# Two edits of a schedule: cached states decayed one by one and loaded in four parts, sample-value products in twos

## The chip, the cores and the metric

The kernel runs on one core of one Trainium2 chip. The metric is the time of one execution on the device in microseconds (us). The core has five engines, each with its own instruction stream worked off in program order: TensorE (PE in the profile, its weight loads as PEld), VectorE (DVE), ScalarE (ACT), GpSimd (POOL) and SyncE (SP), which here mostly issues the DMA transfers. The engines meet through semaphores that the kernel sets and waits for by hand.

## The reference

One inference step of a trunk of two layers, for two groups of requests that share the weights: a prompt of 512 tokens, and 8 samples with 4 new tokens each (32 rows) and cached state. All of it is fp32.

```python
def trunk(x, past_even, past_odd, params):          # called for the prompt and for the samples
    for layer in range(DEPTH):                      # DEPTH = 2
        hn = rmsnorm(x, norm_mix[layer])
        if layer % 2 == 0: mix, st = even_mixer(...)
        else:              mix, st = odd_mixer(hn, odd_w_in[li], odd_w_out[li], past)
        x = x + mix
        hn = rmsnorm(x, norm_mlp[layer])
        x = x + jnp.square(jax.nn.relu(hn @ w_up[layer])) @ w_down[layer]

def ssd_scan(x, dt, a, bm, cm, h0):                 # in even_mixer, chunks of 128 steps
    ...
    def step(h, inp):
        da, s_c = inp
        return h * da[..., None, None] + s_c, h     # the state decays, then the chunk's part is added
    h_last, h_in = lax.scan(step, h0, (exp(acum[:, :, -1]), st))
    y = y + jnp.einsum('bclgn,cbghpn->bclghp', cm, h_in) * jnp.exp(acum)[..., None]

def window_attn_sample(q, k_cat, v_cat, n_past, dil, slopes, sink):   # in odd_mixer, dil = 1, 4, 16
    idx = n_past + jnp.arange(t_len)[:, None] - dil * steps[None, :]
    kg, vg = k_cat[:, idx], v_cat[:, idx]           # cached keys and values gathered by stride
    scores = jnp.einsum('btkgd,btjkd->btkgj', q, kg) * dh ** -0.5 + bias
    p, lse = softmax_lse(scores, sink)
    return jnp.einsum('btkgj,btjkd->btkgd', p, vg), lse
```

Each of the 8 samples has a cached scan state `state_ssm` of 32 heads x 64 x 128, in four groups of 8 heads. In layer 1 the three patterns' results are merged by their softmax denominators.

## The kernel before

**Big products.** Every projection is computed transposed, weights as the stationary operand, 512 + 32 columns as two halves of 272 (`HALF`). Each fp32 product is split into three (high x high, low x high, high x low), which gives six matmuls for one 128 x 128 block of weights. Eight such blocks make a chunk, in a PSUM tile `gp`. The kernel's time is laid out by these chunks: one chunk is a *slot* (`z`), one block in it a *place* (`part`, 0 to 7). All other work is woven in "beside" it: at a place, TensorE issues the six matmuls and then what the tables list for this place; the other engines walk the same tables.

**The scan (lines 115 to 165, `ssd_events`).** During the projection of the query and gate weights (24 slots, 192 places) the scan of layer 0 runs beside it in 20 steps, `SSD[T] = (g, c)`: for each group g of 8 heads first `c == 4`, the samples, which take 14 places from `W = SSD_W[T]` on, then the prompt's four chunks, 7 places each. For `c == 4` the state of all eight samples lies in `hs_t` (128 partitions x 8 samples x 512, 2 MB). TensorE multiplies c by it (`c_times_h`, line 2360) at W and W+1, which needs the loaded states (`hs_in`); its `y_of_sample` (line 2375) comes at W+4; from W+5 on comes one state product per place and sample (`state_of`, line 2389, its matmul line 2403), into one of two PSUM banks in turn. On VectorE, in the order of the tables: `c_h_out` at W+1, samples 0 to 3 of `hs_t` times their decay at W+2 (`decay_of_sample`, line 1708, its instruction line 1713), `y_out_of` at W+4, samples 4 to 7 at W+5, and from W+5 on one addition of a state product to a sample's state per place (`state_of_sample`, line 1716, its instruction line 1719). The state product of sample b waits for the addition of sample b-2 (line 2391), since they share a bank. `st.link(m)` makes VectorE's next instructions wait until m has been written. Between these lie VectorE's other duties: the mask product `m` (line 1658), the chunk's drain (`chunk_out`), x products, weight splits, and gate products (line 1589) of the groups. GpSimd does `c_exp` (lines 2846, 2849) and, per chunk, copies and masks that wait for the row transfers `heads` (line 785). SyncE stores the states at W+14 and loads the next group's at W+22, in one DMA of 2 MB (`load_states`, line 794).

**Layer 1 (lines 286 to 350).** The projection and output products run over 88 slots, in four quarters qd of four heads each, from `SLOT0 = (0, 18, 38, 58)`. The prompt's pieces (scores, turn, values) come at every slot of a quarter. The samples' values are read from the cache as *units*: `unit(U)` = (qd, half, g, t): 18 units a quarter, nine for samples 0 to 3 (half 0) and nine for samples 4 to 7. A unit is one 0.5 MB load of a value tile `vs` (`load_v`, line 958, the DMA's line 973) and one *set* of four products of probabilities and values (`times_unit`, line 2748; line 2759, eight records in the trace). In quarters 0 to 2 there are two value tiles (`N_RING`), in the last 15; a load into a tile waits until the set that used it is done. `sample_units` (line 293) gives each unit its place, every `per` places; each place is followed by one set. From these places follow: `SUM_AT`, where VectorE sums a finished half (`sum_v`, line 2168; it copies the half out of PSUM), `SB_AT`, where the half is turned and split into the operand of the output product (`sb`: TensorE products, ScalarE's `b_hi`, VectorE's `b_lo` on line 2165), and `LOAD_AT`, at which of three turns of a slot SyncE issues each load. The queue order of SyncE in a slot is: value loads of the turns early and mid, one key item (`load_item`, line 945, which itself waits for GpSimd's product of an earlier item), a weight group, value loads of the late turn, a second key item.

**Small products.** `small_events` places the small jobs of a quarter: `rq`, `rk`, `rv` (rows of the samples' queries, keys, values turned by TensorE, line 2697), `vt`, `mg`, `sb` and so on. They share one PSUM bank, and each job's TensorE part waits until the job before it in the table is drained (`small_done`). On VectorE, `factors_out` (line 2123, its copies line 2139) for quarter qd is emitted at the end of slot SLOT0 + 27; the next slot begins with the chunk's drain and, in every other slot, the weight split (line 1999).

## Time and profile before

The median of the three runs is 2426.38 us (2424.07 to 2429.6). The rows below and in the last section but one come from one profiled execution.

| | |
|---|---|
| time of the profiled execution | 2428.49 us |
| span from the first to the last instruction | 2426.7 us, 41530 instructions |
| granted TensorE clock, mean | 0.963 of full speed |
| TensorE matmuls (PE) busy | 2250.9 us, 93% |
| weight loads (PEld), beside them | 2101.6 us, 87% |
| VectorE | 1383.7 us, 57% |
| ScalarE | 730.9 us, 30% |
| GpSimd | 430.0 us, 18% |
| chain that ended last | PE 69%, DVE 12%, DMA 7%, issue 5%, ACT 4%, POOL 2% |
| DMA | 519.92 MB, mean 214 GB/s, best of the 40 slices 324 GB/s |

The chain that ended last is followed back from the last instruction, at each step to what released it. A share of 69% for TensorE says that for the rest of the span something else decided when the next TensorE instruction could start. Busy shares are means over stages with different limits: in the scan VectorE has far more to do per slot than in the MLPs.

### The profile page before, as it was taken

The page shows a single profiled execution, that of the slowest core. Times are in us where ns is not written, and L with a number is a line of the kernel's source. Part 1 is how long each engine was busy: PE and PEld are TensorE (multiplying, and loading weights), DVE is VectorE, ACT ScalarE, POOL GpSimd, SP SyncE. Part 2 cuts the span into 40 slices and gives each one's busy share as a digit, 9 for nine tenths or more (in the row PEclk, how much of TensorE's full clock was granted, in tenths as well). Part 3 has the DMA queues.
Part 4 walks back from the last instruction along what each step waited for, and adds up shares of the span by engine and source line. Part 5 has one row for each costly group of instructions (what it writes and reads, how often), then busy time and mean ns, then how long its engine had stood idle before and what let it go on. Part 6 is the DMA issues. An engine that isn't in the chain of part 4 may idle for free.

```text
span 2426.7 us, 41530 instructions
## 1 busy us (share of the span) xinstructions
PE 2250.9 (93%) x17512; PEld 2101.6 (87%) x17512; DVE 1383.7 (57%) x2005; ACT 730.9 (30%) x1408; POOL 430.0 (18%) x287
## 2 busy tenths in 40 slices
PE   7998887888899999999999999999999979999997
PEld 7988776677688999999998987898898858999997
DVE  4786777785644544344565564665646647353444
ACT  3323324355333322122313322323232224221221
POOL 1000322211121100000035434244324400000000
PEclk9999998888999999999999999999999989999999
DMA  4225766771233687787758668569657945877874
GB/s 164 70 81 179 242 242 229 263 234 62 79 134 121 227 269 260 260 276 252 252 165 300 223 225 297 167 199 313 215 172 254 324 156 173 271 264 246 278 260 176
DMA packets 282909, 519.92 MB, mean 214 GB/s; under 512 B 17776, under 2 KB 253664, under 8 KB 278880
## 3 DMA queue, kind: packets, MB, share of 16 engines
q1 hardware_dynamic: 271408, 324.44, 40.9%
q10 hardware_dynamic: 5888, 177.91, 20.0%
q0 software_dynamic: 5440, 15.08, 1.7%
q8 instruction: 131, 2.15, 0.4%
q14 instruction: 42, 0.34, 0.0%
HBM read 483.76 MB, written 210.80 MB: 286 GB/s over the span
## 4 chain that ended last, share of the span: by engine, by line
PE 69%; DVE 12%; DMA 7%; issue 5%; ACT 4%; POOL 2%; SPq 0%; DVEq 0%; ACTq 0%; POOLq 0%
PE gp L2264 33%; PE gp L2797 14%; PE gp L2593 5%; PE gp L2417 4%; DMA uk<-in_dil_k 3%; DVE cacc L1556 2%; DMA decay<-tmp_a_row 2%; PE mp L2684 2%; POOL uq L2897 1%; DMA vs<-in_dil_v 1%; PE mp L2653 1%; PE mp L2759 1%; PE mp L2515 1%; ACT w_hi L1004 1%; PE mp L2533 1%
## 5 line engine op out<-in xcount | busy, mean ns | idle before, releaser
L2264 PE MATMUL gp<-a_hi,w_hi 128*128 128x272 f32 x1456 | 307.0, 292 | 23.3 <-DVE w_lo L1479 12.1
L2264 PE MATMUL gp<-a_lo,w_hi 128*128 128x272 f32 x1456 | 303.2, 290 | 0.0
L2264 PE MATMUL gp<-a_hi,w_lo 128*128 128x272 f32 x1456 | 302.2, 289 | 0.0
L2897 POOL TENSOR_TENSOR uq<-uq,uk 128x1024 f32<-128x1024 f32 x96 | 249.6, 2604 | 293.9 <-DMA uk<-in_dil_k 293.8
L2797 PE MATMUL gp<-a_hi,w_hi 128*128 128x272 f32 x1152 | 261.1, 308 | 0.0
L2264 PEld LDWEIGHTS gp<-a_hi,w_hi 128*128 128x128 f32 x1456 | 231.8, 190 | 26.4 <-DVE cin L1545 13.2
L2797 PE MATMUL gp<-a_lo,w_hi 128*128 128x272 f32 x1152 | 240.5, 291 | 0.0
L2797 PE MATMUL gp<-a_hi,w_lo 128*128 128x272 f32 x1152 | 240.4, 290 | 0.0
L2264 PEld LDWEIGHTS gp<-a_hi,w_lo 128*128 128x128 f32 x1456 | 230.9, 190 | 0.0
L2264 PEld LDWEIGHTS gp<-a_lo,w_hi 128*128 128x128 f32 x1456 | 229.1, 190 | 0.0
L2264 PE MATMUL gp<-b_lo,w_hi 128*128 128x272 f32 x1024 | 212.1, 289 | 0.0
L2264 PE MATMUL gp<-b_hi,w_hi 128*128 128x272 f32 x1024 | 211.7, 288 | 0.0
L2264 PE MATMUL gp<-b_hi,w_lo 128*128 128x272 f32 x1024 | 211.2, 288 | 0.0
L2797 PEld LDWEIGHTS gp<-a_hi,w_hi 128*128 128x128 f32 x1152 | 180.7, 192 | 27.0 <-issue 25.2
L1779 DVE TENSOR_TENSOR x_t<-x_t,gp 128x544 f32<-128x544 f32 x88 | 63.3, 719 | 223.5 <-PE gp L2264 189.6
L1308 ACT ACTIVATE w_hi<-w_raw 128x2048 fp32r<-128x2048 f32 x63 | 120.1, 1906 | 230.4 <-PE gp L2264 230.4
L2797 PEld LDWEIGHTS gp<-a_hi,w_lo 128*128 128x128 f32 x1152 | 183.6, 191 | 0.0
L2797 PEld LDWEIGHTS gp<-a_lo,w_hi 128*128 128x128 f32 x1152 | 182.6, 191 | 0.0
L1945 DVE TENSOR_TENSOR w_lo<-w_raw,w_hi 128x2048 fp32r<-128x2048 f32 x62 | 142.1, 2292 | 69.5 <-ACT w_hi L1308 69.5
L2264 PEld LDWEIGHTS gp<-b_hi,w_hi 128*128 128x128 f32 x1024 | 161.1, 188 | 0.0
L2264 PEld LDWEIGHTS gp<-b_hi,w_lo 128*128 128x128 f32 x1024 | 160.9, 188 | 0.0
L2264 PEld LDWEIGHTS gp<-b_lo,w_hi 128*128 128x128 f32 x1024 | 159.9, 189 | 0.0
(384 smaller groups left out, 4090.9 us busy)
## 6 DMA issues: line engine op xcount, KB each, us to landing
out_dil_ks<-in_dil_k ACTq DMA_DIRECT2D x32, 2044.0 KB
out_dil_vs<-in_dil_v ACTq DMA_DIRECT2D x32, 2044.0 KB
uq<-tmp_rows SPq DMA_DIRECT2D x96, 512.0 KB, 6.5
w_raw<-in_odd_w_in SPq DMA_DIRECT2D x36, 1024.0 KB, 7.9
vs<-in_dil_v SPq DMA_DIRECT2D x67, 512.0 KB, 7.1
w_raw<-in_w_up SPq DMA_DIRECT2D x32, 1024.0 KB, 8.2
w_raw<-in_w_down SPq DMA_DIRECT2D x32, 1024.0 KB, 8.0
uk<-in_dil_k SPq DMA_DIRECT2D x64, 512.0 KB, 7.4
```

The source lines that it names most:

```text
L1004: nc.scalar.activation(w_hi[:, s1], w_raw[:, s1], ACT.Copy, scale=scale).then_inc(w_hi_done, 1)
L1308: nc.scalar.activation(w_hi[:, s1], w_raw[:, s1], ACT.Copy, scale=scale).then_inc(w_hi_done, 1)
L1556: ins = nc.vector.scalar_tensor_tensor(out=cacc[:, c, 0:COUT], in0=cin[:, c, j:j + COUT], scalar=wb[:, 0, j:j + 1], in1=cacc[:, c, 0:COUT] ...
L1779: nc.vector.tensor_tensor(xc, xc, gp[:, n % 2, :, 0:HALF], ALU.add).then_inc(drained, 1)
L1945: nc.vector.tensor_tensor(w_lo[:, s1], w_raw[:, s1], w_hi[:, s1].bitcast(F32), ALU.subtract).then_inc(w_lo_done, 1)
L2264: m = nc.tensor.matmul(gp[:, c, h, 0:HALF], w[:, sl, k, c * P:(c + 1) * P], x[:, k, h * HALF:(h + 1) * HALF], start=n < 2, stop=n >= 46)
L2417: m = nc.tensor.matmul(gp[:, c, h, 0:HALF], w[:, G % 2, part, c * P:(c + 1) * P], x[:, part, h * HALF:(h + 1) * HALF], start=part == 0 and ...
L2515: m = nc.tensor.matmul(mp[:, 1, j * P:(j + 1) * P], at_e[:, p % 2, j], at_f[:, p % 2, tile], start=True, stop=True)
L2593: m = nc.tensor.matmul(gp[:, c, h, 0:HALF], w[:, G % 2, part, c * P:(c + 1) * P], x[:, h * HALF:(h + 1) * HALF], start=part == 0 and j == ...
L2684: m = nc.tensor.matmul(out, pt1[:, j], v[:, at, f], start=(n == 0), stop=(n == len(rows) - 1))
L2797: m = nc.tensor.matmul(gp[:, gc, h, 0:HALF], w[:, k, n * P:(n + 1) * P], x[:, k, h * HALF:(h + 1) * HALF], start=k == 0 and j == 0, stop=k ...
L2897: nc.gpsimd.tensor_tensor(uqs[n % 3], uqs[n % 3], k, ALU.mult).then_inc(item_mul, 1)
```

## The change

In the scan, `decay_of_sample` handles one sample and is called eight times: samples 0 and 1 at W+2, and sample b+2 right behind the addition of sample b, at W+5+b. Each call waits for its own instruction (`st.link`), where before the last of four did. The load of the next group's states is issued as four DMAs of two samples (0.5 MB) each, at W+21, W+23, W+25 and W+27, in place of one of 2 MB at W+22; the first group's load, ahead of the stage, is four DMAs too, and TensorE waits for all four.

In layer 1, two units share a place: five places a half (2, 2, 2, 2 and 1 units) in place of nine, 40 in place of 72 in all. The distance between them is 9, 11, 11 and 4 places in the four quarters, before 5, 6, 6 and 2. With the places, everything that is derived from them moves: the first half's `sb` from (28, 3), (47, 3), (67, 3) to (27, 3), (46, 3), (66, 3), given as (slot, place); the second half's from (34, 3), (54, 3), (74, 3), (86, 3) to (33, 3), (53, 3), (73, 3), (85, 3); the sums with them; and the turns at which SyncE issues the value loads.

```diff
--- before.py
+++ after.py
@@ -138,16 +138,19 @@
             for r in range(2):
                 at(pe, W + r, "c_h", T, r)
             at(dve, W + 1, "c_h", T, 0)
-            at(dve, W + 2, "decay_s", T, 0)
+            for b in range(2):
+                at(dve, W + 2, "decay_s", T, b)
             at(pe, W + 4, "y_s", T, 0)
             at(dve, W + 4, "y", T, 0)
-            at(dve, W + 5, "decay_s", T, 1)
             for b in range(NB):
                 at(pe, W + 5 + b, "state_s", T, b)
                 at(dve, W + 5 + b, "state_s", T, b)
+                if b + 2 < NB:
+                    at(dve, W + 5 + b, "decay_s", T, b + 2)
             at(sp, W + 14, "store_s", g, 0)
-            if g < 3:
-                at(sp, W + 22, "load_s", g + 1, 0)
+            for k in range(4):
+                if g < 3:
+                    at(sp, W + 21 + 2 * k, "load_s", g + 1, k)
         else:
             st = W - 1
             at(pe, st, "state", T, 0)
@@ -294,8 +297,8 @@
 
     at, turned = {}, {}
     for qd, b in enumerate(SLOT0):
-        per = (5, 6, 6, 2)[qd]
-        places = [(b + 22 + (n + 1) // 8, (n + 1) % 8) for n in (per * u + 6 * (u >= N_HALF) for u in range(N_UNITS))]
+        per = (9, 11, 11, 4)[qd]
+        places = [(b + 22 + (n + 1) // 8, (n + 1) % 8) for n in (per * (5 * (u // N_HALF) + u % N_HALF // 2) for u in range(N_UNITS))]
         for u in range(N_UNITS):
             at[N_UNITS * qd + u] = places[u]
         first, last = places[N_HALF - 1], places[-1]
@@ -791,18 +794,18 @@
                 src = scratch["a_row"][8 * g:8 * g + 8, c * P:c * P + w].rearrange("(o h) l -> o h l", o=1)
                 sp.dma_start(decay[:, T % 3, :, 0:w], src.to_broadcast([P, 8, w])).then_inc(heads_in[T % 3], 16)
 
-            def load_states(g):
+            def load_states(g, k):
 
                 wait(sp, hs_out, 16 * g)
-                sp.dma_start(hs_t[:].rearrange("p b h e -> p (b h e)"),
-                             a["h0"][g:g + 1].rearrange("o n b f -> n (o b f)")).then_inc(hs_in, 16)
-
-            def beside(what, n):
+                sp.dma_start(hs_t[:, 2 * k:2 * k + 2].rearrange("p b h e -> p (b h e)"),
+                             a["h0"][g:g + 1, :, 2 * k:2 * k + 2].rearrange("o n b f -> n (o b f)")).then_inc(hs_in, 16)
+
+            def beside(what, n, k=0):
 
                 if what == "heads":
                     heads(n)
                 elif what == "load_s":
-                    load_states(n)
+                    load_states(n, k)
                 elif what == "store_s":
                     sp.wait_ge(state_done, n_state(5 * n, NB - 1))
                     sp.dma_start(o["ssm_s"][n:n + 1].rearrange("o n b f -> n (o b f)"),
@@ -832,7 +835,8 @@
             load_group("q", 1)
             sp.wait_ge(a_ready, KC)
             sp.wait_ge(ssq_done, KC)
-            load_states(0)
+            for k in range(4):
+                load_states(0, k)
             for z in range(N_PROJ):
                 if z % 2 == 0 and z < N_PROJ:
                     n = z // 2 + 2
@@ -853,8 +857,8 @@
                         sp.wait_ge(out_done, 16 * 19)
                         for T in range(3):
                             heads(T)
-                    for what, n, _ in SSD_SP.get(8 * z + part, ()):
-                        beside(what, n)
+                    for what, n, k in SSD_SP.get(8 * z + part, ()):
+                        beside(what, n, k)
                     if 8 * z + part in GATE_P:
                         load_z(GATE_P.index(8 * z + part))
                     if (z, part) == (22, 2):
@@ -1705,13 +1709,11 @@
                 dve.wait_ge(st_mm, n_state(T))
                 nc.vector.tensor_tensor(new, new, inc, ALU.add).then_inc(state_done, 1)
 
-            def decay_of_sample(T, half):
+            def decay_of_sample(T, b):
 
                 g = SSD[T][0]
                 dve.wait_ge(c_h_mm, g + 1)
-                for b in range(4 * half, 4 * half + 4):
-                    m = nc.vector.tensor_tensor(hs_t[:, b], hs_t[:, b], cols(eas[:, b, 8 * g:8 * g + 8], P), ALU.mult)
-                st.link(m)
+                st.link(nc.vector.tensor_tensor(hs_t[:, b], hs_t[:, b], cols(eas[:, b, 8 * g:8 * g + 8], P), ALU.mult))
 
             def state_of_sample(T, b):
 
@@ -2363,7 +2365,7 @@
                 if r == 0:
                     wait(pe, state_done, 12 * g)
                     pe.wait_ge(c_msk_done, g + 2)
-                    pe.wait_ge(hs_in, 16 * (g + 1))
+                    pe.wait_ge(hs_in, 64 * (g + 1))
                 for j in range(4):
                     b = 4 * r + j
                     m = nc.tensor.matmul(mp[NS * j:NS * j + NS, 3, :], c_msk[:, NS * b:NS * b + NS],
```

## Rows read from the trace of the kernel before

**Rows 1.** Busy us by engine, sum of the samples' four stretches

```profile
sum 85.00, PE 62.42 PEld 56.79 DVE 80.83 ACT 23.30 POOL 22.37; mean PE 15.61 PEld 14.20 DVE 20.21 ACT 5.82 POOL 5.59
```

**Rows 2.** TensorE's waits, 1385-2012 us: us, times, longest

```profile
PE mp L2759 <- DMA vs<-in_dil_v: 10.9, 6, 3.1
...
PE mp L2697 <- DVE b_lo L2165: 3.3, 3, 1.2
```

**Rows 3.** VectorE's timeline, group 0: start, us, line, tiles [idle before <-releaser]

```profile
245.87 2.48 DVE L1713 TENSOR_TENSOR hs_t<-hs_t,eas 128x512 f32<-128x512 f32 x4
...
249.58 6.84 DVE L1713 TENSOR_TENSOR hs_t<-hs_t,eas 128x512 f32<-128x512 f32 x4
256.45 1.28 DVE L1719 TENSOR_TENSOR hs_t<-hs_t,mp 128x512 f32<-128x512 f32 x2
...
264.18 0.69 DVE L1719 TENSOR_TENSOR hs_t<-hs_t,mp 128x512 f32<-128x512 f32 x1 [0.29 <-PE mp L2403]
```

**Rows 4.** GpSimd's timeline, group 0

```profile
250.12 2.38 POOL L2846 TENSOR_TENSOR decay<-decay,consts 128x1024 f32<-128x1024 f32 x1 [16.61 <-ACT c_exp L1095]
252.46 2.80 POOL L2849 TENSOR_TENSOR c_exp<-c_exp,xbc 128x1024 f32<-128x1024 f32 x1
```

**Rows 5.** TensorE's timeline, group 0

```profile
257.19 0.54 PE L2403 MATMUL mp<-x_end,b_msk 96*128 96x512 f32 x1 [4.79 <-DVE hs_t L1719]
257.53 0.66 PE L2417 MATMUL gp<-a_hi,w_hi 128*128 128x272 f32 x2
...
261.03 0.42 PE L2417 MATMUL gp<-a_hi,w_hi 128*128 128x272 f32 x2
...
262.01 0.41 PE L2417 MATMUL gp<-a_hi,w_hi 128*128 128x272 f32 x2
...
264.93 0.70 PE L2405 MATMUL mp<-x_end,b_row 128*128 128x512 f32 x1
```

**Rows 6.** VectorE's timeline, group 3

```profile
470.35 4.44 DVE L1589 TENSOR_TENSOR xbc<-xbc 128x544 f32<-128x544 f32 x4
```

**Rows 7.** TensorE's timeline, group 3

```profile
482.39 1.13 PE L2405 MATMUL mp<-x_end,b_row 128*128 128x512 f32 x2 [1.21 <-DVE hs_t L1719]
```

**Rows 8.** GpSimd's timeline, ahead of group 3

```profile
450.70 0.21 POOL L2841 COPY c_msk<-xbc 128x32 f32<-128x32 f32 x1 [18.08 <-DMA decay<-tmp_a_row]
```

**Rows 9.** TensorE's timeline, a single set in quarter 0, sixteen products in quarter 3

```profile
1385.10 0.41 PE L2797 MATMUL gp<-a_lo,w_hi 128*128 128x272 f32 x2
1385.45 0.64 PE L2759 MATMUL mp<-vs,p_all 128*32 128x256 f32 x8
...
1386.38 0.42 PE L2797 MATMUL gp<-a_hi,w_lo 128*128 128x272 f32 x2
1386.63 0.41 PE L2797 MATMUL gp<-a_lo,w_hi 128*128 128x272 f32 x2
...
1970.59 1.07 PE L2759 MATMUL mp<-vs,p_pad 128*32 128x256 f32 x16
```

**Rows 10.** SyncE's and TensorE's timelines, value loads in quarter 0

```profile
1474.38 0.61 SPq L973 DMA_DIRECT2D vs<-in_dil_v  x1
...
1482.41 0.66 PE L2759 MATMUL mp<-vs,p_pad 128*32 128x256 f32 x8 [3.11 <-DMA vs<-in_dil_v]
...
1492.46 0.64 PE L2759 MATMUL mp<-vs,p_pad 128*32 128x256 f32 x8 [1.68 <-DMA vs<-in_dil_v]
```

**Rows 11.** VectorE's timeline, slot 46 and slots 65 and 66

```profile
1630.22 3.63 DVE L1999 TENSOR_TENSOR w_lo<-w_raw,w_hi 128x2048 fp32r<-128x2048 f32 x1
...
1822.09 7.23 DVE L2139 COPY fbx<-fs 32x4 f32<-32x4 f32 x16
...
1830.66 2.82 DVE L1999 TENSOR_TENSOR w_lo<-w_raw,w_hi 128x2048 fp32r<-128x2048 f32 x1
```

**Rows 12.** TensorE's timeline, `rq` of slots 46 and 66

```profile
1630.13 0.38 PE L2697 MATMUL mp<-ident,q_t 128*32 128x128 f32 x2
...
1830.56 0.38 PE L2697 MATMUL mp<-ident,q_t 128*32 128x128 f32 x2 [1.71 <-DVE q_t L2050]
```

## The prediction

> **What bounds the kernel now.** I read four views, in this order. The page first: in its list of engines TensorE leads with 93% of the span, and it leads the chain that ended last too (both in the table of the profile), so what an edit is worth is read from the stretches in which TensorE stands still. Then the stretches that the diff touches. In the scan, the four stretches in which the samples' states are handled last 85 us together; TensorE is busy for 62.4 us of them and VectorE for 80.8 us [rows 1]. There VectorE is the bound, and its row is the one to count. In layer 1 TensorE is the bound, and what interrupts it are waits for value tiles and for VectorE [rows 2]. Last the timelines of single engines, with the emission order in the code beside them, since every engine works in program order.
>
> Sums are made in us against the profiled execution (2428.49 us, span 2426.7); the median of the runs shown is 2426.38, so 2.1 us come off at the end. A *place* is one eighth of a slot: six matmuls of the big product, three pairs whose starts lie 0.25 us apart at full clock [rows 9]: 0.75 us.
>
> **Decays one by one (groups 0 to 3 of the scan).** Nothing is removed: eight decays, eight adds as before. What moves is their order, and each decay is now followed by a wait for itself (8 such waits in place of 2).
>
> Before, group 0: four decays run while VectorE waits for the y product at 245.87 [rows 3], so they are nearly free. The next four take 6.84 us where four alone take 2.48 [rows 3]. GpSimd has two operations there, from 250.12 and 252.46 [rows 4], so each decay that meets one waits for its end or is stretched. The Trainium skill (SBUF — State Buffer, Who interferes with whom) says that a VectorE instruction with two SBUF inputs and a GpSimd one that reads SBUF exclude each other, and that one with a single SBUF input isn't touched. By that rule, the trace agrees: the decays (both inputs in SBUF) stretch to 6.84 us for four, and the adds, which read PSUM, keep 0.64 to 0.69. Without such a lock, a decay would cost 0.62 wherever it stood, and this part would come to its self-waits alone. TensorE meanwhile stands still for 4.79 us, waiting for the first add [rows 5]. That looks like the prize, but the last add ends at 264.87 and the product behind it starts at 264.93 [rows 3, 5]: VectorE had almost no idle time in between, so it decides when the stretch ends.
>
> After, group 0: two decays to 247.1, then VectorE idles until y (1.2 us of free cover lost); y to 249.6; add 0 to 250.55; decay 2 waits out GpSimd's first operation, to 253.05; add 1; decay 3 waits out the second, to 255.9. Left are six adds and four decays at 0.60, two x products and the chunk's drain of the same width (1.8), the mask product of twice that width (1.1; estimates from the adds' 0.64 [rows 3]) and four self-waits (an estimate, 0.06 each: twice the 0.03 us that lie between the last decay's end at 256.42 and the first add, which does wait, at 256.45 [rows 3]). That is 9.2 us: the last add ends at 265.1. **+0.3.** TensorE's one long stall becomes several short ones of the same sum. Group 1 has the same picture, +0.3. In group 2 a weight split delays both orders alike, +0.1.
>
> Group 3: here the four gate products lie between the adds, and the last of them ends at 470.35 + 4.44 = 474.79 [rows 6]. Before, all decays were done by then; the adds that were left followed, and the state product started at 482.39 after waiting for the last one [rows 7]. After, decays 4 to 7 come behind the gates: 4 x 0.60 + 4 x 0.06 = 2.6, and the gates end some 0.3 later, as a blocked decay comes ahead of them. **+3.0.** Sum of this part **+3.7**. Bounds: no gain above VectorE's idle time in the four stretches, 85.0 - 80.8 = 4.2 [rows 1]; a loss up to +7, if TensorE's low clock, now spent inside the stall, falls behind the stretch in two groups. Its price: after 4.79 us of idling the granted clock is at the lower of its two levels, 1.2 GHz (a pair then takes 0.66 us in place of 0.42 [rows 5]), and two places with their state products take 3.50 us (257.53 to 261.03), one at the upper level 0.98 (261.03 to 262.01) [rows 5]: 3.50 - 2 x 0.98 = 1.5 us.
>
> **The load in four parts.** Bytes are the same, issues 4 for 1, each no longer than the 0.61 us of a 0.5 MB load [rows 10], on a queue that only waits there. What it moves past: the row transfers `heads`, a weight load, `store_chunk`. In group 3 GpSimd waited 18.08 us for the `heads` transfer [rows 8], since that stands behind 2 MB in the queue. Now it stands before the last quarter; 0.5 MB at the page's best slice (324 GB/s, in the table) is 1.6 us, of which I let 1 reach the end, since TensorE has other work. **-1.** The two ends: -4.5, a quarter of the 18.08, if all of it was on the path; +2, if the last quarter lands its 1.6 us after the c-times-h product wants it.
>
> **Products in twos.** Between the starts of the pairs ahead of and behind a set lie 1386.38 - 1385.10 = 1.28 us, two pairs' 0.50 taken off leaves 0.78 for a single set. Sixteen in a row take 1.07 where eight take 0.64, so a second set costs 0.43 [rows 9]. A merge saves 0.35. There are 32; 8 lie in the last quarter, where TensorE waits for ScalarE anyway. 24 x 0.35 = **-8.4**, fully on TensorE's path.
>
> Against it stand the loads. In quarters 0 to 2 the ring has two buffers, so a pair is refilled only when both sets are done, and both refills are one behind the other. The load issued at 1474.38 is held by the key item before it, not by its buffer; TensorE waited 3.11 us for it at 1482.41 (slot 31, place 5) and 1.68 us for the next at 1492.46 (slot 32, place 2) [rows 10]. In the new order two loads stand at this point of SyncE's queue, and both serve slot 31, place 1. The second, issued 0.6 later, lands at about 1483.5, 1.1 after the first; the next pair's single load follows from 1485 with 8 us of landing and is there at 1493.4, 0.9 after 1492.46. From there the old order has two more sets (1.6) and 0.2 of waiting, the new one none: quarter 0 ends 0.9 earlier, where the merges alone would give 8 x 0.35 = 2.8. The waits eat 1.9, and one spell of the low clock behind a wait of some 10 us about half of its 1.5: +2.7. For quarters 1 and 2, with the load ahead of the last place at the same point of the queue as before and wanted one to three places sooner, +0.5 each. **+3.7**, on top of 10.9 us of such waits [rows 2].
>
> Then the sums and splits of the samples' halves (`sum_v`, `sb`), whose places follow. (a) The second half's `sb` goes from slot 34, 54, 74 to 33, 53, 73, to the very place of an `rv`. The 3.3 us in which a transpose waited for `b_lo` of line 2165, 1.1 each [rows 2], go; `rv`, now behind it in the same place, waits half of that each time (an estimate: the same round over ScalarE and VectorE, begun sooner). **-1.8.** (b) The first half's `sb` goes from slots 47 and 67, place 3, to 46 and 66, place 3. All small products share one PSUM bank and wait for the one before, so `rq` at place 7 now waits for `sb`'s `b_lo`, and that stands on VectorE behind `factors_out` of slot 45, the drain and the weight split of slot 46. The split ran to 1630.22 + 3.63 = 1633.85; in quarter 2 `factors_out` ended at 1829.32 and the split at 1833.48 [rows 11]. `sum_v` is now ahead of `factors_out` and waits for place 5 of slot 45; with that and its own work I put `b_lo` 1.6 and 1.9 us behind the split (an estimate, two or three VectorE steps of the 0.6 us that a decay takes). So it ends near 1635.4 and 1835.4, while TensorE wants `rq` at about 1630.0 and 1828.7: before it started at 1630.13 and 1830.56, the second with a wait of 1.71 [rows 12]. 5.4 + (6.7 - 1.7) = **+10.4**, and the low clock after both, 2 x 1.5 = **+3.0**. Who waits behind: the rest of slot 46, all on TensorE.
>
> Last quarter: two sets (0.78 + 0.43) now lie between the transpose and the next score product, which is the path there, and `sb` no longer stands behind `factors_out`, for which I take off 0.7 (an estimate): **+0.5**.
>
> Sum: 3.7 - 1 - 8.4 + 3.7 - 1.8 + 10.4 + 3.0 + 0.5 = **+10.1**. 2428.5 + 10.1 = 2438.6, and 2.1 less for the median: **2436.5 us**.
>
> **Rivals.** *The decays pay (0.12).* TensorE stands still for 85.0 - 62.4 = 22.6 us of the four stretches [rows 1], and if GpSimd's operations then fall beside the adds, VectorE gains up to its 4.2 us and the waits at 46 and 66 are half as long. -4 - 1 - 8.4 + 3.7 - 1.8 + 5 + 0.5 = -6: about 2420, down to 2415. For it: the long row of 6.84. Against: two GpSimd operations block two decays in either order. *The bank's wait is covered (0.18).* ScalarE and VectorE are early enough in slots 46 and 66, for instance as GpSimd's pattern there changes; then 10.4 + 3.0 shrinks to about 3: near 2426. For it: `factors_out` is long only because of GpSimd (7.23 for sixteen copies [rows 11]). *Value tiles decide, much slower (0.10).* SyncE's queue is full in the second halves, and each of the five pairs of a second half waits 2 us more than reckoned: 2443 to 2448. The point from which it decides is a landing above 10 us. *The edit doesn't do what it says:* the places follow from the formula in the diff, so no chance is left for it.
>
> **How the numbers follow.** Forecast 0.60, rivals 0.12, 0.18, 0.10. A measurement of this kernel can tell about 0.2%, 4.9 us, from no change. Faster (below 2421.5): the first rival and a little of the second, 0.13. Within: most of the second and 0.06 of the forecast's lower edge, 0.22. Slower: 0.65. The range takes in the second rival and the bounds of the scan part, and leaves out most of the first and the top of the third: 2422 to 2446.
>
> **What would show it.** Right: the stall of 4.79 is gone, short ones at line 2403 add up to the same, and the state product of the next chunk starts within 0.5 us of where it did from the stretch's start (3 us later in group 3); `rq` of slots 46 and 66 waits over 4 us for `b_lo`; the stretch of 18 sets costs 0.35 x 8 less per quarter apart from waits. Wrong: VectorE's stretches in the scan are shorter than before by over 1 us each, or `rq` doesn't wait there.

## The result and the profile after

The changed kernel is slower: 2447.72 us (median, 2443.78 to 2448.65) beside 2427.99 us for the kernel before, a ratio of 1.0079 with a 95% interval of 1.0054 to 1.0105. A second set of runs on another chip gave 2443.26 beside 2427.35 us, 1.0053 (1.0033 to 1.0073). So by the ratios the loss is 13 to 19 us. The forecast was 2436.5 us, +10.1, with a range to 2446: the sign was right, the size was not. The first set lies inside the band of the prediction's third rival (2443 to 2448), but its mechanism isn't what the traces show (see the step on value loads).

| profiled execution | before | after |
|---|---|---|
| its own time, us | 2428.49 | 2443.78 |
| span, us | 2426.7 | 2442.0 |
| granted TensorE clock, mean | 0.963 | 0.956 |
| TensorE matmuls busy, us | 2250.9 | 2257.3 |
| VectorE busy, us | 1383.7 | 1380.6 |
| ScalarE busy, us | 730.9 | 731.5 |
| GpSimd busy, us | 430.0 | 431.8 |
| instructions | 41530 | 41559 |

The work is the same; 15 us more of waiting and of low clock lie between it. TensorE's waits between 1380 and 1970 us, after (us in total, times, longest). Before, those for value tiles were 10.9 us, and those of a transpose for `b_lo` 3.3 [rows 2]:

```profile
PE mp L2761 <- DMA vs<-in_dil_v: 14.0, 5, 5.9
PE mp L2699 <- DVE b_lo L2167: 9.9, 2, 5.1
```

**Where the time went.** The two programs issue the same VectorE instructions that drain the big product's chunks, in the same order. The start of each of them in one trace less its start in the other gives the lead or lag at that point, and the difference of two such lags what a stretch cost. One pair of traces is not enough for this: in layer 1 two kernels with the same code there differ by up to 6 us in a quarter, as the transfers fall. So I take every trace of this study, 18 with that of before, one for each kernel or second set, and compare for each stretch those that have an edit in it with those that don't (means, in us against the trace of before, ± the standard error of the difference):

| stretch of the trace before, us | edit in it | with it | without | difference | forecast |
|---|---|---|---|---|---|
| 225 to 445, scan groups 0 to 2 | decays one by one | -2.0 (10 traces) | +0.1 (8) | -2.1 ± 0.4 | +0.7 |
| 445 to 516, scan group 3 | decays one by one | +4.6 (5) | +0.2 (12) | +4.4 ± 0.3 | +3.0 |
| 409 to 461, the load | in four parts | -1.3 (6) | -1.0 (12) | -0.3 ± 0.4 | -1 |
| 1382 to 1576, quarter 0 | sets in twos | +5.0 (9) | +1.5 (9) | +3.4 ± 1.1 | -0.7 |
| 1576 to 1949, quarters 1 and 2 | twos, `sb` moved | +2.6 (6) | -3.3 (7) | +5.9 ± 1.5 | +7.6 |
| 1949 to 2049, quarter 3 | twos | +5.1 (4) | +1.3 (12) | +3.8 ± 1.2 | +0.5 |
| sum | | | | +15.1 | +10.1 |

The forecast's column is its own terms, shared out: the merges at 2.8 a quarter, the value waits at 2.7, 0.5 and 0.5, the second half's `sb` at -0.6 each. Traces with only part of an edit are in neither column: `after_group3_fours` in group 3, the five that have twos and leave `sb` in quarters 1 and 2, the two with the sum late in quarter 3. The load's stretch overlaps the two beside it, so its -0.3 is counted in part twice. Elsewhere (516 to 1382 us, and from 2049 us on) the kernels don't differ: +0.1 ± 0.7, and nothing. The sum of 15.1 agrees with the measured 13 to 19. It also says where the forecast failed: not in the term on which I had staked most (the waits of `rq`), but in quarters 0 and 3, which I had put near nothing (+3.4 for -0.7, +3.8 for +0.5).

### The profile page after: what moved, and what is told of

Same layout as the page of the kernel before. It is cut to its first block, busy times and chain, and to the rows that moved or that the text cites. A ratio compares the mean times of both kernels' runs of the same rounds, so it can differ in the third digit from the quotient of the medians.

```text
span 2442.0 us, 41559 instructions
## 1 busy us (share of the span) xinstructions
PE 2257.3 (92%) x17512; PEld 2111.3 (86%) x17512; DVE 1380.6 (57%) x2005; ACT 731.5 (30%) x1408; POOL 431.8 (18%) x287
## 3 DMA queue, kind: packets, MB, share of 16 engines
q8 instruction: 131, 2.15, 0.4%
## 4 chain that ended last, share of the span: by engine, by line
PE 68%; DVE 14%; DMA 7%; issue 5%; ACT 4%; POOL 2%; SPq 0%; DVEq 0%; ACTq 0%; POOLq 0%
PE gp L2266 32%; PE gp L2799 13%; PE gp L2595 5%; DMA uk<-in_dil_k 4%; PE gp L2419 4%; DVE cacc L1560 2%; DMA decay<-tmp_a_row 2%; POOL uq L2899 2%; PE mp L2686 1%; PE mp L2761 1%; PE mp L2655 1%; PE mp L2517 1%; PE mp L2665 1%; ACT w_hi L1008 1%; DMA vs<-in_dil_v 1%
## 5 line engine op out<-in xcount | busy, mean ns | idle before, releaser
L2799 PEld LDWEIGHTS gp<-a_hi,w_hi 128*128 128x128 f32 x1152 | 180.2, 191 | 18.7 <-issue 16.6
```

The costliest lines, as they stand in the source:

```text
L2799: m = nc.tensor.matmul(gp[:, gc, h, 0:HALF], w[:, k, n * P:(n + 1) * P], x[:, k, h * HALF:(h + 1) * HALF], start=k == 0 and j == 0, stop=k ...
```

## The experiments

All against the kernel before on the same chip; the interval is about 0.2% either way, some 5 us, so the traces carry most of the weight where parts are compared. The ratio is an estimate from all runs of both kernels, not the quotient of the two medians, from which it differs by up to 0.16%. Where the text gives a kernel's gain or loss in us, it is this ratio times the median of before.

| kernel | median, us | before, us | ratio (95% interval) |
|---|---|---|---|
| `a_decays` | 2426.52 | 2423.80 | 1.0010 (0.9987 to 1.0033) |
| `b_parts` | 2426.05 | 2423.80 | 1.0005 (0.9988 to 1.0022) |
| `c_quarters012` | 2433.09 | 2423.80 | 1.0026 (1.0009 to 1.0044) |
| `c_quarter3` | 2429.19 | 2423.80 | 1.0018 (0.9998 to 1.0037) |
| `c3_sum_late` | 2431.71 | 2427.99 | 0.9999 (0.9977 to 1.0021) |
| `a_groups012` | 2425.68 | 2427.99 | 0.9978 (0.9958 to 0.9998) |
| `c012_sb_late` | 2431.95 | 2427.99 | 1.0010 (0.9989 to 1.0032) |
| `mended` | 2433.36 | 2427.99 | 1.0007 (0.9986 to 1.0028) |
| `after_again` | 2443.26 | 2427.35 | 1.0053 (1.0033 to 1.0073) |
| `after_sum_late` | 2441.12 | 2427.35 | 1.0063 (1.0043 to 1.0084) |
| `after_quarter3_ones` | 2442.98 | 2427.35 | 1.0062 (1.0043 to 1.0080) |
| `after_group3_fours` | 2439.43 | 2427.35 | 1.0047 (1.0030 to 1.0064) |
| `c012_both_late` | 2431.68 | 2425.81 | 1.0024 (1.0003 to 1.0045) |
| `c12_both_late` | 2429.36 | 2425.81 | 1.0019 (0.9999 to 1.0038) |
| `best` | 2427.47 | 2425.81 | 0.9999 (0.9983 to 1.0015) |
| `a_groups012_again` | 2421.95 | 2422.80 | 0.9983 (0.9964 to 1.0003) |

The four parts alone add up to 1.0059 (+14 us), inside what the two sets of the whole gave. So the times show no effect of one part on another, though four intervals of 0.2% each would hide one of several us.

### One part at a time

`a_decays` has the edits of `ssd_events` and `decay_of_sample` of the diff alone. 

> The decays one by one alone. Theory T (the two traces): the last sample stretch, group 3, loses what the first three don't: its state product starts about 2 us later, at the low clock, and the scan ends 4 to 5 us later than before; the whole kernel +4 to +5 us. The prediction's step: +3.7. Rival R (the offset in the scan comes from the load in four parts): within 1 us of before.

`b_parts` has the load alone. 

> The load in four parts alone. Theory T: -1 to 0 us, the GpSimd wait for the row transfer ahead of group 3 is a few us shorter than 18.08. Rival R (the load makes the scan late): +3 us or more.

The two sets can't tell either from before. The traces can. With the decays one by one the stretch of group 3 costs +4.3 (`a_decays`) and from +3.9 to +5.5 in the four traces of the changed kernel that keep them there; without, -0.4 to +1.3. That is theory T's 4 to 5 us, and the load isn't its cause (rival R; `b_parts` has -0.4 there). The load's own step is small. GpSimd's wait for the row transfer ahead of group 3 follows (the number in brackets), in the timeline of the kernel after and in that of `b_parts` ([rows 8] show 18.08 before), and then, from the list of DMA issues between 400 and 460 us after, the state loads, with the us from issue to landing at the end:

```profile
448.59 0.48 POOL L2843 COPY c_msk<-xbc 128x32 f32<-128x32 f32 x1 [15.40 <-DMA decay<-tmp_a_row]
```

```profile
450.49 0.21 POOL L2843 COPY c_msk<-xbc 128x32 f32<-128x32 f32 x1 [17.16 <-DMA decay<-tmp_a_row]
```

```profile
hs_t<-in_h SPq DMA_DIRECT2D x4, 512.0 KB, 23.7
```

Against the one trace of before the wait looks 1 to 3 us shorter, but in the twelve traces with the load in one DMA it is 16.4 to 18.7 us, and `b_parts` with 17.16 lies among them. The like compare better: of the ten traces with the decays one by one in groups 0 to 2, the five with the load in parts wait 15.3 to 15.5 us and the other five 16.4 to 16.6. That is 1 us, and none of it reaches the end: either five run 1.6 us ahead in the stretch from 409 to 461 us. The 0.5 MB quarters took 23.7 us to land in the trace after and 16.9 in `b_parts`; what they wait for, and so what is left of GpSimd's wait, was not tested.

`c_quarters012` and `c_quarter3` have the places of the diff in some quarters alone:

```diff
-        per = (5, 6, 6, 2)[qd]
+        per = (9, 11, 11, 2)[qd]      # c_quarters012; c_quarter3: (5, 6, 6, 4)
-        places = [... for n in (per * u + 6 * (u >= N_HALF) for u in range(N_UNITS))]
+        places = [... for n in (per * (5 * (u // N_HALF) + u % N_HALF // 2) if qd < 3
+                                else per * u + 6 * (u >= N_HALF) for u in range(N_UNITS))]
```

> Products in twos in quarters 0 to 2 alone, the last quarter as before. The prediction's steps give -8.4 + 3.7 - 1.8 + 10.4 + 3.0 = +6.9 us, with rq of slots 46 and 66 waiting over 4 us each. Theory T (the two traces, slot by slot): those waits are there, but most of their time is given back before the quarter ends, so +2 to +4 us, nearly all of it in quarter 0.

> Products in twos in the last quarter alone. The prediction's step gives +0.5 us. Theory T: +6 to +9 us, all of it between the first set of the last quarter and the last output group; TensorE's products there run in part at the lower clock level and the last wait of TensorE, for the factors, grows from 5.6 to 7.7 us. Rival (the trace showed drift): within 1 us of before.

`c_quarters012` came out at +6.3 us (+2.2 to +10.7), near the forecast's +6.9, and `rq` waited 5.48 and 5.11 us. The interval still holds most of theory T's +2 to +4; it is the traces that speak against T's reason, that these waits are given back before the quarter ends. I had read it off one pair of traces. From 1639 to 1742 us the changed kernel gains 3.9 us on the trace of before, but so do the kernels with nothing changed there (-2.4 to -3.4 in the six of them); it was the trace of before that was late in that stretch. `c_quarter3` cost +4.4 us (-0.5 to +9.0), in its trace +4.7 where those with that quarter as before are within 0.13 of zero in eight of twelve. The low clock and the last wait (7.69 us) are as theory T has them, its +6 to +9 us is too much, and by the trace the forecast's +0.5 is wrong; the time alone would allow it.

### The last quarter

Between two turns of the prompt's pieces (line 2663) TensorE runs a score product, value products and sets; the turn waits for ScalarE's `e`, which waits for VectorE, which waits for the score product. Before, and in `c_quarter3` (same lines):

```profile
1977.26 0.66 PE L2663 MATMUL mp<-ident,e 128*128 128x128 f32 x4 [0.77 <-ACT e L1349]
1977.85 1.16 PE L2653 MATMUL mp<-k_t,q_t 64*128 64x128 f32 x8
...
1982.50 0.65 PE L2663 MATMUL mp<-ident,e 128*128 128x128 f32 x4 [0.51 <-ACT e L1349]
```

```profile
1978.18 0.66 PE L2663 MATMUL mp<-ident,e 128*128 128x128 f32 x4 [1.08 <-ACT e L1349]
1978.77 0.64 PE L2759 MATMUL mp<-vs,p_all 128*32 128x256 f32 x8
1979.22 0.61 PE L2759 MATMUL mp<-uk,p_pad 128*32 128x256 f32 x8
1979.77 1.16 PE L2653 MATMUL mp<-k_t,q_t 64*128 64x128 f32 x8
...
1984.42 0.66 PE L2663 MATMUL mp<-ident,e 128*128 128x128 f32 x4 [0.51 <-ACT e L1349]
```

From score product to next turn it is 4.65 us in both. The two sets now stand in front of the score product, on that chain, and the round takes 6.24 in place of 5.24 us. The three last rounds are 5.26, 5.23, 5.26 us before and 5.43, 6.23, 5.43 with twos: +1.35. Of that I had reckoned 1.2.

Behind the last round comes VectorE's own chain. Its timeline before, and after:

```profile
1985.63 0.69 DVE L2081 TENSOR_REDUCE st<-e 128x2 f32<-128x512 f32 x1
1987.73 2.86 DVE L2116 COPY bx<-st 32x8 f32<-32x8 f32 x16 [1.42 <-ACT e L1349]
...
1991.09 0.42 DVE L2174 COPY se_t<-mp 128x256 f32<-128x256 f32 x1
```

```profile
1998.84 0.69 DVE L2083 TENSOR_REDUCE st<-e 128x2 f32<-128x512 f32 x1
2002.00 0.42 DVE L2176 COPY se_t<-mp 128x256 f32<-128x256 f32 x1 [2.47 <-PE mp L2761]
2002.34 2.85 DVE L2118 COPY bx<-st 32x8 f32<-32x8 f32 x16
```

The last half's sum (`se_t`) has passed ahead of the factors (`bx`), as the last set's place moved from one slot into the slot before, and makes them wait for TensorE's last set. `c3_sum_late` and `after_sum_late` put it back behind them:

```diff
-        SUM_AT.setdefault((_s, when(_p)), []).append(_u)
+        SUM_AT.setdefault((_s, when(_p)) if _u < 4 * N_UNITS - 1 else (_s + 1, "early"), []).append(_u)
```

> Products in twos in the last quarter alone, but VectorE sums the last half one table entry later, behind the copies of the factors instead of ahead of them. Theory T1 (the last quarter's cost is that VectorE's factors wait for TensorE's last set): TensorE's last wait falls from 7.7 us to about 5.6, the two rounds of the output transposes are back at the upper clock level, and the time from the last turn to the first output group is as before: about +1.5 us is left of the +4.7 of the last quarter, all in the score rounds. Theory T2 (the cost is the grouping itself, in the rounds): the last wait changes by under 1 us and +4 us or more stays.

> The changed kernel with VectorE's last sum of the last quarter behind the copies of the factors. Theory T1 (that order costs): TensorE's last wait before the output transposes is 5.7 us in place of 7.7, 1 to 2 us less than the changed kernel in the last quarter, more if the clock comes back sooner. Rival T2 (the low clock alone decides there): no difference in the quarter beyond what two executions of the same order differ by.

TensorE's wait ahead of the output transposes, after and in `c3_sum_late` (before: 5.58):

```profile
2011.54 2.05 PE L2741 MATMUL mp<-ident,o_q 128*128 128x128 f32 x8 [7.71 <-DVE o_q L2151]
```

```profile
1999.24 2.05 PE L2739 MATMUL mp<-ident,o_q 128*128 128x128 f32 x8 [5.72 <-DVE o_q L2149]
```

The wait is back, as T1 has it, but only 0.5 us come from it (from the last turn to this product: 10.23 before, 10.82 with twos, 10.31 with the sum late), because TensorE's last set ends that much earlier against the chain. The quarter keeps +3.1 and +3.3 us in the two traces with the sum late, for +3.9, +3.9, +4.7 and +7.9 in the four without. The clock did not come back sooner: the first half of the second group of output transposes takes 2.07 us, the low level, in either, and 1.16 before. The whole group lasts 3.6 to 3.8 us in all six traces with twos; with sets one by one it lasts 2.05 us in ten traces and 3.7 in two (`c12_both_late`, `best`). So most of the quarter's cost is accounted for: 1.35 us in the rounds, 0.6 from the last turn to the transposes and 1.7 in the transposes, 3.65 where two of the four traces have 3.8. T1 is right on the order and wrong on its weight. The whole-kernel times don't settle more: 0.9999 and 1.0018 for the two single ones, 1.0063 and 1.0053 for the two full ones, each pair inside its intervals.

**The clock there.** In the trace after the last round but one takes 9.98 us. Busy times in that round (first the window, then its length, then TensorE's; the granted clock is the third number from the right), before and after, and then in a slow round of `mended`, whose last quarter is that of before; it is the fourth round from the end:

```profile
1977.00:1983.00 6.00, 5.22 (x64) 4.10 (x64) 1.62 (x3) 2.23 (x10) 0.00 (x0) 1.00 0.05 16
```

```profile
1985.00:1991.00 6.00, 6.00 (x51) 4.21 (x52) 1.27 (x2) 0.60 (x1) 0.00 (x0) 0.53 0.02 8
```

```profile
1966.00:1972.00 6.00, 6.00 (x35) 3.83 (x33) 1.43 (x2) 0.60 (x1) 0.00 (x0) 0.50 1.00 321
```

In three of the twelve traces with sets one by one (`mended`, `c12_both_late`, `best`: +4.9, +5.5, +4.3) this fourth round from the end ran at the lower level, 8.84 us for 5.6 to 6.2 in the other nine. So a round can fall to 1.2 GHz whatever the grouping. Whether twos make it likelier can't be said from six traces. It isn't what makes the quarter's mean: without the four traces that have such a round, twos cost +3.8, +3.8 and +4.7 us, and the nine others +0.1 in the mean.

`after_quarter3_ones` is the changed kernel with this quarter as before. 

> The changed kernel with the products of the last quarter one by one as before. If the last quarter's share is what quarter 3 alone showed (+4.4 us): 4 to 8 us less than the changed kernel, rounds of 5.26, 5.23 and 5.26 us and a last wait of 5.6 us. By the prediction's +0.5 for the last quarter: no difference.

 Its trace has the rounds of before, the last wait of 5.59 and -0.1 us in the quarter; its time (1.0062, against 1.0053) doesn't show the 4 us, which the two intervals are wide enough to hide. The trace supports it, the times leave it open.

### Group 3 of the scan

`a_groups012` and `after_group3_fours` keep the old two calls where g is 3:

```diff
+            if g < 3:
+                for b in range(2):
+                    at(dve, W + 2, "decay_s", T, b)
+            else:
+                at(dve, W + 2, "decay_s", T, -1)      # samples 0 to 3
...
+            if g == 3:
+                at(dve, W + 5, "decay_s", T, -2)      # samples 4 to 7
```

> Decays one by one in groups 0 to 2, in group 3 four by four as before. Theory T (the loss of the decays lies in group 3 alone): the trace has no +4.7 us between 445 and 516 us; by that point it stands within 1 us of before or up to 2 us ahead, and the whole kernel comes 0 to 3 us earlier than before. Rival (the prediction's +0.3 a group): +0.7.

> The changed kernel with the decays of group 3 four by four as before. If the loss of the decays lies in group 3 alone: 4 to 5 us less than the changed kernel, all between 445 and 516 us. By the prediction's step for group 3: 3 us less.

The end of group 3 on VectorE and TensorE, after:

```profile
480.71 2.29 DVE L1470 TENSOR_TENSOR w_lo<-w_raw,w_hi 128x2048 fp32r<-128x2048 f32 x1
482.92 1.28 DVE L1721 TENSOR_TENSOR hs_t<-hs_t,mp 128x512 f32<-128x512 f32 x2
...
484.25 2.07 PE L2407 MATMUL mp<-x_end,b_row 128*128 128x512 f32 x2 [2.87 <-DVE hs_t L1721]
```

and TensorE's line in `after_group3_fours`:

```profile
482.08 1.13 PE L2414 MATMUL mp<-x_end,b_row 128*128 128x512 f32 x2 [2.15 <-DVE hs_t L1728]
```

A weight split of 2.29 us stands ahead of the last two additions. The decays that now come behind the gates push it back by 1.85 us (from 478.86, before); TensorE, with its own work done, waits 2.87 where [rows 7] have 1.21, and its clock is down when it goes on: the state product takes 2.07 us for 1.13. Of this stretch's +4.4, the part from 478 to 488 us is +3.2 to +3.5 in each of the five traces with the decays one by one in this group, and 0.0 in each of the thirteen others. In each of the five, 0.7 of it lies ahead of the state product and the rest, 2.4 to 2.8 us, behind it, where the clock is low. In the trace of `after_group3_fours` the part ahead of it costs +2.3, since GpSimd's two operations fell into the second four decays (a row of 6.81 us, where [rows 3] show the same of group 0); so it saved 2 us of the 4 to 5, and its time of 1.0047 beside 1.0053 tells no more.

`a_groups012` is what is left of the change that gains: groups 0 to 2, -2.1 us in the traces. A second set of it: 

> Decays one by one in groups 0 to 2, group 3 four by four, once more. The first set gave 0.9978 (0.9958 to 0.9998), 5 us, of which the trace shows under 2 us in the scan. If the gain is real, 0.997 to 0.999 again; if it was the spread of layer 1 from execution to execution, 0.999 to 1.001.

 The two gave 0.9978 and 0.9983, -5.3 us (-0.5 to -10.2) and -4.1 us (-8.7 to +0.7). The traces explain 2 of these; the rest is no larger than the intervals.

### Quarters 0 to 2: the bank, the order or the queue

`c012_sb_late` leaves the first half's `sb` at slots 28, 47, 67; `mended` is that and `a_groups012` together:

```diff
-        turned[qd, 0] = (first[0] + 1, 3) if qd < 3 else (first[0], 7)
+        turned[qd, 0] = (first[0] + 2, 3) if qd < 3 else (first[0], 7)
```

> Products in twos in quarters 0 to 2, with the first half's turn and split (sb) left at its old places, slots 28, 47 and 67, place 3. By the prediction's sum, 10.4 + 3.0 us go away with the waits of rq in slots 46 and 66, so 6.9 - 13.4 = -6.5 us against before; those two waits are 1.7 us or less. Rival (waits in layer 1 are given back, what counts is the DMA queue): the same +6 us as with the moved sb.

> Both together: decays one by one in groups 0 to 2, products in twos in quarters 0 to 2 with the first half's sb at its old places; the load in one DMA, the last quarter and group 3 as before. If the parts add up, -6.5 - 1.5 = -8 us, about 0.997 of before. Rival (values and keys from the DMA queue set the pace of layer 1): within 2 us of before.

`c012_sb_late` measured +2.4 us (-2.7 to +7.8), not -6.5, and `mended` 1.0007 (0.9986 to 1.0028), not 0.997. In `c012_sb_late` the two waits of `rq` are still there, for another tile:

```profile
PE mp L2697 <- DVE q_t L2050: 6.6, 2, 3.4
```

I took the sum for the culprit, as it stands ahead of `factors_out` on VectorE and so ahead of the drain that writes `q_t`. `c012_both_late` puts it back as well, `c12_both_late` does that with quarter 0 one by one, and `best` adds `a_groups012`:

```diff
+        _first = _u // N_UNITS < 3 and _u % N_UNITS < N_HALF
-        SUM_AT.setdefault((_s, when(_p)), []).append(_u)
+        SUM_AT.setdefault((_s + 1, "early") if _first else (_s, when(_p)), []).append(_u)
```

> Products in twos in quarters 0 to 2, with both the first half's sum (sum_v, back behind factors_out) and its sb at their old places. Theory S (the sum ahead of factors_out holds VectorE's whole row up, q_t included, which is why moving sb back alone left waits of 3.3 us): the waits of rq on q_t in slots 46 and 66 fall from 6.6 us together to about 2 (before: 1.7), and the kernel comes 3 to 5 us earlier than with sb alone moved back: -2 us against before. Rival Q (GpSimd's products and the DMA queue hold the row up): the two waits stay above 5 us together and the time is that of sb alone moved back, +2.4 us.

> The same in quarters 1 and 2 alone, quarter 0 as before. It tells what is left of the twos in the quarters where the value loads are not yet late: 16 merges of 0.35 us are -5.6, the loads +1 and the second half's sb -1.2: -5.8 us by the prediction's terms. Theory L (in quarter 0 the value loads eat the gain): 2 us or more ahead of the kernel with quarter 0 in twos as well. Rival: the same as that one, so that the loads of quarter 0 cost nothing beyond its merges.

> Decays one by one in groups 0 to 2 and products in twos in quarters 1 and 2 with the first half's sum and sb at their old places; all else as before. If the parts add up: -2 us in groups 0 to 2 and -3 to -6 in the quarters, 0.997 to 0.998 of before. Rival (layer 1 moves by some us from execution to execution whatever is done to it, and the twos save nothing there): 0.999 to 1.001.

```profile
PE mp L2698 <- DVE q_t L2051: 5.7, 2, 2.9
```

Rival Q stands on this: 5.7 us, not 2, and a time of 1.0024 where theory S had -2 us. The sum's place isn't the cause. As far as the traces show (no run changes it), what paces VectorE in slots 45 and 46 is its chain of small copies, from `bx` to `fbx`, which GpSimd's products stretch. In slots 45 and 65 it takes 14.2 to 15.2 us from the first `bx` to `q_t` in all 22 cases with twos and in ten of the 14 without, and 11.8 to 12.7 us in the other four, in three of which two GpSimd operations fall into it and not three. The end of it in the trace after:

```profile
1631.06 5.04 DVE L2141 COPY fbx<-fs 32x4 f32<-32x4 f32 x16
...
1637.12 3.15 DVE L2001 TENSOR_TENSOR w_lo<-w_raw,w_hi 128x2048 fp32r<-128x2048 f32 x1
1640.19 0.18 DVE L2167 TENSOR_TENSOR b_lo<-mp,b_hi 128x32 fp32r<-128x32 f32 x1
```

A TensorE that comes sooner, because it has fewer breaks (from 1576 to 1616 us it gains 0.3 to 0.8 us in ten of the eleven traces with twos), waits for it longer: for `q_t` 2.8 to 3.4 us where the kernels of ones wait up to 2.3, and for `b_lo`, two VectorE entries later, 4.9 to 5.9. By stretches, slot 46 and its neighbours (1616 to 1639 us) cost +5.1 ± 0.6 with `sb` moved and +2.6 ± 0.7 with it at the old place, slot 66 (1815 to 1840 us) +5.0 ± 0.4 and +2.5 ± 0.5. So moving `sb` costs 5 us in the two together, and the twos themselves another 5 there, which is more than their merges save. Quarters 1 and 2 as a whole: +5.9 ± 1.5 with `sb` moved, +1.9 ± 1.9 without.

**What a merge saves.** [rows 9] gave 0.35 us, and the trace after has the same for a pair between matmuls of the big product: 1411.42 - 1409.46 = 1.96 less three pairs of 0.25 is 1.21, and 2 x 0.78 - 1.21 = 0.35.

```profile
1409.46 0.41 PE L2799 MATMUL gp<-a_lo,w_hi 128*128 128x272 f32 x2
1409.81 1.07 PE L2761 MATMUL mp<-vs,p_pad 128*32 128x256 f32 x16
...
1411.42 0.41 PE L2799 MATMUL gp<-a_lo,w_hi 128*128 128x272 f32 x2
```

But of the 54 sets of quarters 0 to 2 before only 27 stood so. The others stood at a place with another small product, where the break is paid already, as here (before):

```profile
1473.73 0.50 PE L2684 MATMUL mp<-v_row,pt 128*128 128x64 f32 x3
1474.15 0.64 PE L2759 MATMUL mp<-vs,p_pad 128*32 128x256 f32 x8
1474.72 0.52 PE L2797 MATMUL gp<-a_hi,w_hi 128*128 128x272 f32 x2
```

Such a set costs 0.57 us, the time from its start to the next. 27 x 0.78 + 27 x 0.57 = 36.5 us before; after there are 18 free pairs (1.21), 6 beside others (1.00), 5 free single sets and 1 beside others: 32.3. The merges save 4.2 us, half of the forecast's 8.4.

**Quarter 0.** The wait for value tiles at slot 31, place 1, after:

```profile
1486.06 1.08 PE L2761 MATMUL mp<-vs,p_pad 128*32 128x256 f32 x8 [5.94 <-DMA vs<-in_dil_v]
1487.54 1.08 PE L2761 MATMUL mp<-vs,p_pad 128*32 128x256 f32 x8 [0.40 <-DMA vs<-in_dil_v]
```

where [rows 10] have 3.11 and 1.68. The nine traces with twos in this quarter wait 6.9 us for values in the mean, the others 4.4: +2.5, of which the forecast had 1.9. With merges worth 1.4 a quarter, half a low-clock spell (0.8; behind the wait a set takes 1.08 us for 0.64) and the -0.6 of `sb` this makes +1.3; the stretch shows +3.4 ± 1.1. The 2 us between them stay open. `c12_both_late` beside `c012_both_late` gives 1.0019 and 1.0024, too close to tell; the quarter's traces, +0.2 and +9.5, point to theory L but are single executions.

`best` ended level with the kernel before (0.9999), not at 0.997 to 0.998; in its trace the last quarter costs +4.3 us, by a round at the low clock and the transposes behind. No combination with twos beats before.

## Why the prediction was right and wrong, step by step

- **"VectorE decides when the stretch ends" (groups 0 to 2), +0.3 a group.** The picture held closely: after, additions and decays interleave, two of the decays are blocked and the last addition ends at 265.30, forecast 265.1:

```profile
249.68 0.69 DVE L1721 TENSOR_TENSOR hs_t<-hs_t,mp 128x512 f32<-128x512 f32 x1 [0.27 <-PE mp L2405]
250.28 2.52 DVE L1716 TENSOR_TENSOR hs_t<-hs_t,eas 128x512 f32<-128x512 f32 x1
252.84 0.69 DVE L1721 TENSOR_TENSOR hs_t<-hs_t,mp 128x512 f32<-128x512 f32 x1
253.44 2.17 DVE L1716 TENSOR_TENSOR hs_t<-hs_t,eas 128x512 f32<-128x512 f32 x1
...
263.90 1.40 DVE L1721 TENSOR_TENSOR hs_t<-hs_t,mp 128x512 f32<-128x512 f32 x2
```

  Group 0 itself costs +0.2 ± 0.2, as forecast. The sum was still off by 2.8: it is -2.1, not +0.7. "Group 1 has the same picture" failed, and so did its neighbour for group 2: they gain 0.7 ± 0.2 and 0.5 ± 0.3, and another 1.0 ± 0.3 comes behind group 2, up to 445 us. I had worked out one group and copied it. In group 1 the picture differs by the second blocked decay: 1.50 us for group 0's 2.17 in all ten traces, about the size of the 0.7. What gains that last 1.0 was not tested, and it needn't be the decays: from 410 to 445 us all ten traces with them are 1.4 to 1.6 us ahead, but so are three of the eight without. Of the signs named, the stall of 4.79 us became four waits of 0.30 to 2.75 us, 3.8 together, and the next chunk's state product starts at 265.45, 0.5 us later.
- **Group 3, +3.0.** Right in place and mechanism, the term mis-sized: +4.4. The decays moved behind the gates do come late, but against the lag at 445 us the state product slips by 2.1 us only in the mean of the five traces (1.6 to 2.8). The low clock, which I had kept in the bounds ("falls behind the stretch in two groups") and out of the sum, adds 2.4 to 2.8 us behind it.
- **The load, -1.** -0.3 ± 0.4. That GpSimd waits less is right, by 1 us and not by a quarter of its wait; that 1 us reaches the end is not shown.
- **Merges, -8.4 "fully on TensorE's path".** Mis-sized twice: 4.2 us, because half of the sets had no break of their own, and what TensorE saved it waited out in slots 46 and 66.
- **Value loads, +3.7.** The loads' term was near in quarter 0 (+2.5 us of waiting for 1.9) and too small in quarters 1 and 2, where the waits rose by 1.7 and 1.2 us for 0.5 each: 5.4 us in all for 2.9. The third rival's "2 us more than reckoned" for each pair of a second half isn't there, so that the first set fell into its band is chance.
- **Quarter 0, -0.7: the largest miss.** +3.4 ± 1.1. Of the 4.1 us, 1.4 are the merges' size and 0.6 the waits; 2 us stay open.
- **`sb` of the second half, -1.8.** The waits on `b_lo` of line 2165 in `rv`'s places (3.3 us) did go; what came for them is 1.5 us (three times 0.5), as forecast.
- **`rq` waits for `b_lo`, 5.4 and 6.7 us.** Shown in every trace with `sb` moved: 4.85 to 5.88 and 4.94 to 5.27. In the trace of `c_quarters012`, `b_lo` ended at 1639.2, which is 1635.4 and its lag of 3.7 us at slot 45. That the end agrees is luck: the weight split ended 1.5 us later than reckoned, and `b_lo` came right behind it and not 1.6 us later. The low clock behind them, 3.0, is at most half of that: the matmuls are at 0.66 us a pair for a few places only. Together +5.9 ± 1.5 for the two quarters, for 7.6: the best of the large terms, and that by luck in part. The stretches around the two slots cost 10.1 us for the 13.4 of the waits and the clock, but moving `sb` is only 5 of them; the other 5 are the twos' own, which no term of mine had.
- **The last quarter, +0.5: the step that failed.** +3.8 ± 1.2. I had weighed the sets between turn and score product (1.2 us, found: 1.35) and then taken 0.7 off for `sb`, where the profile shows the reverse: the last sum passed ahead of the factors (0.5 us), TensorE's wait grew, and 1.7 us went to the lower clock in the second group of output transposes, in all six traces with twos. The change of the sum's place stood in the tables; I had followed it in quarters 1 and 2 and not here.
- **The range.** Its upper end took in the bounds of the scan part and left out the top of the rival on value tiles. It had no case in which spells of low clock in the scan and in the last quarter add up, though the price of one (1.5 us) was in the text; the excess in group 3 and half of that in the last quarter are such spells.

## What to carry to other kernels

Where VectorE or another engine is behind TensorE, time saved on TensorE can turn into a longer wait, and that into a lower clock: here two slots took back more than the merges saved. A merge is worth its price only where nothing waits next. When places are derived from a formula, list every table that follows from it and walk through each quarter, the last above all, since nothing hides work there. And a stretch must be compared over several executions of each kernel: one pair of traces gave me a "gain that is given back" which was the lateness of one trace.

## What the runs showed of the hardware

TensorE's granted clock in the same code differed from execution to execution: one round of the last quarter with the same instructions took 5.6 to 6.2 us in nine traces and 8.8 us, at 1.2 GHz, in three. In group 3 the clock was down behind a wait of 2.87 us in all five traces that have it, and up behind 1.21 and 2.15 us at the same place. The price of a wait need not be its length: 1.66 us more of waiting there made the 10 us around it 3.3 us longer.

In group 0 two VectorE decays met a GpSimd operation each, in either order of issue: they took 2.87 and 2.83 us before and 2.52 and 2.17 after, in place of 0.69. In the trace after each of them ended 0.54 us behind the end of GpSimd's operation (252.26 and 255.07). The addition between them, of the same size but reading PSUM, kept 0.69. The Trainium skill (SBUF — State Buffer, Who interferes with whom) says that an instruction with two SBUF inputs, as a decay, and a GpSimd one that reads SBUF use a port that only one of them can hold; the traces agree.
